# The row turns and queries of tile 1 placed behind the third head's scores, and the first copy of the rows made by ScalarE

## The chip, the cores and the metric

The kernel runs on one core of a Trainium2 chip. The metric is the device time of one launch in microseconds (us), the median of the runs taken; lower is better.

## The reference, cut to what matters

One layer of a decoder for 512 prompt rows and 8 sample rows of width 1024, all in float32: an input projection, a chunked gMLP mixer, a gated linear attention mixer, their merge with a layer norm that gives x1, and then the channel mixer PEER, a second layer norm and a small gated embedding. The part around which the kernel is built is PEER:

```python
q = (xb @ w_q).reshape(blk, PEER_HEADS, 2, half)      # 8 heads of queries, each half normalised
s = jnp.einsum('thpd,hpnd->thpn', q, keys_f)          # scores against 2 x 128 keys per head
s1, i1 = lax.top_k(s[:, :, 0], 16);  s2, i2 = lax.top_k(s[:, :, 1], 16)
sc, ci = lax.top_k(cand, 16)                          # 16 of the 256 sums; idx = expert numbers
h = jax.nn.gelu(jnp.einsum('thkd,td->thk', u_tab[idx], xb))
y = jnp.einsum('thk,thkd->td', softmax(sc) * h, v_tab[idx])
```

Each token takes 16 rows of u_tab and 16 rows of v_tab (4 KB each) for each of 8 heads, so the 512 prompt rows gather 512 x 128 rows from each of two tables of 16384 rows.

## The kernel before, in words

The prompt is four tiles of 128 tokens (0 to 3), the eight sample rows are a fifth (NT = 4). Group 0 is tiles 0 and 1, group 1 is tiles 2, 3 and the samples. The mixers of group 0 run first. Then the PEER stage begins for tile 0, and all that is left of the kernel's dense work (the queries of tile 1, the whole of the mixers of group 1) is dealt out between its steps.

**The plan.** `plan()` writes one list of events, PLAN. TensorE (PE), VectorE (DVE), ScalarE (ACT) and the SyncE queue (SP) each walk this list in order and do their own part of each event; GpSimd (POOL) has a loop of its own that issues the gathers. The PEER stage has one step for each tile and head (`ITERS` = 32 steps), and each step has 16 slots: slot (n, k) of the plan holds `("dots", n + 1, k)`, so a slot (-1, k) is that of dot (0, k). `behind` is the table of the dense work by slot; `spread_over` deals a list of events evenly, by `cost`, over the slots from a first to a last one. `choices_at` gives the slots of the routing of each head: `route` parts 0 and 1 normalise the queries (statistics on DVE, square root and scaling on ACT, lines 868 and 873), `q turn` transposes them on PE (line 1538) and copies them on ACT (line 884), `scores` multiplies by the keys on PE (line 1548) and copies on ACT (line 892), and parts 2 to 6 are top-16, softmax and index arithmetic on DVE.

**A dot.** `dot(n, k)` (line 1280) multiplies 128 gathered rows of u_tab (one per token, 512 KB, one gather of POOL at line 712) by the tile's rows x1 and sums: one DVE instruction. The rows x1 of a tile are first copied into PSUM (`XD`, line 1276, DVE). There are 6 buffers for u rows at first, and two more from dot (1, 3) on; a gather waits (`u_used`) for the dot that last used its buffer. The gathers of v_tab (line 721) have 8 buffers at first; the ninth waits (`v_used`) for the first `sums` event, the PE matmuls (line 1575) that weigh the v rows into Y. That gather stands in POOL's order at (1, 9), ahead of the further u gathers.

**Jobs.** A job is one PE product into one of three PSUM banks `PJ`, with its evacuation by ACT or DVE. Of interest here: `t1` of tile 1 (two jobs of 4 transposes of x1, line 1492, copied by ACT at line 822), `wq` (16 matmuls for one head's queries of a tile, line 1406, copied by ACT at line 805) and the jobs of `mixers(1)` (lines 1514 and 1390 above all). SP loads the weights in a ring of four 1 MB blocks, each load waiting for the last job that uses the block it replaces (line 567); the transposed x of group 1 (line 619) is loaded after job `("job", 0, "wq", 1, 1)`, the second of tile 1's queries.

The part of `plan()` that places the work, up to the change:

```python
close += [e for j in TILES[1] for e in turn(1, "t1", j)]
wq2 = queries(1)
behind = spread_over(wq[3:PH] + turn(0, "t1", 1) + wq[PH:] + mixers(1) + close + wq2[:1], (-1, 0), (13, 6))
```

`wq[3:PH]` are the queries of heads 3 to 7 of tile 0, `turn(0, "t1", 1)` the row turns of tile 1, `wq[PH:]` the eight query jobs of tile 1.

Of the kernel before, what the change touches and what calls it, by code (L numbers as in the profile page):

```python
# [9 lines left out]
ACT = mybir.ActivationFunctionType  # L10
# [10 lines left out]
PH, NK, TOPK = 8, 128, 16  # L21
# [35 lines left out]
def rows(j):  # L57

    return 128 if j < NT else S
# [79 lines left out]
def out_rows(g):  # L139

    return [("job", g, "wo", i, j) for i in range(4) for j in TILES[g]]


def queries(g):

    return [("job", g, "wq", i, j) for i in range(PH) for j in TILES[g]]
# [12 lines left out]
def spread_over(events, first, last):  # L159

    table, total, run = {}, sum(cost(e) for e in events), 0.0
    start = first[0] * TOPK + first[1]
    n = last[0] * TOPK + last[1] - start + 1
    for e in events:
        at = start + min(int(run / total * n), n - 1)
        table.setdefault(divmod(at, TOPK), []).append(e)
        run += cost(e)
    return table


def turn(g, name, j):

    return [("job", g, name, half, j) for half in range(2)]
# [45 lines left out]
def plan():  # L219

    x1 = [[("x1", j, part) for part in range(2)] for j in range(NT + 1)]
    wo = [[("job", 0, "wo", i, j) for i in range(4)] for j in TILES[0]]
    wq = [("job", 0, "wq", i, j) for j in TILES[0] for i in range(PH)]
# [4 lines left out]
    close = out_rows(1) + [e for j in TILES[1] for e in x1[j]]  # L228
    close += [e for j in TILES[1] for e in turn(1, "t1", j)]
    wq2 = queries(1)  # L230
    behind = spread_over(wq[3:PH] + turn(0, "t1", 1) + wq[PH:] + mixers(1) + close + wq2[:1], (-1, 0), (13, 6))
    behind.update(spread_over(wq2[1:], (13, 10), (15, 15)))
    behind.setdefault((END, 10), []).append(("order", NT - 1))
    for k, e in enumerate(spread_norm("norm2")):
# [155 lines left out]
def decoder_step(nc, x_all, x_t, state, p_t, w_blk, w_gkl, w_gk, b_gk, ws_t, ws0, b_s, lnv_g, lnv_b, gn_g,  # L390
                 w_o, ln1_g, ln1_b, w_q, keys_t, u_tab, v_tab, ln2_g, ln2_b, w_pe, w_pg,
                 y_all, st_p, st_s, cv_p, cv_s):
    with ExitStack() as ctx:
        def sem(name):
            return ctx.enter_context(nc.semaphore(name))
# [33 lines left out]
        x1 = at(O_X1, NT + 1, D)  # L429
# [60 lines left out]
        def q_of(j, h):  # L490
# [33 lines left out]
        XD = ctx.enter_context(nc.psum_tensor("XD", [128, 1024], F32))  # L524
# [11 lines left out]
        pj_done, pj_act, pj_dve = sem("pj_done"), sem("pj_act"), sem("pj_dve")  # L536
        soft_part, mid_ok, fac_ok, ent_ok, e_ok, qk_ok = (sem(n) for n in (
            "soft_part", "mid_ok", "fac_ok", "ent_ok", "e_ok", "qk_ok"))
        clear_ok = sem("clear_ok")
        att_ok, s_ok, ms_ok, sdo_ok, on_ok, kpad_ok, qpad_ok, s0_new = (sem(n) for n in (  # L540
            "att_ok", "s_ok", "ms_ok", "sdo_ok", "on_ok", "kpad_ok", "qpad_ok", "s0_new"))
        var_ok, sd_ok, vn_ok, m_ok, x1_ok, x2_ok = (sem(n) for n in ("var_ok", "sd_ok", "vn_ok", "m_ok", "x1_ok", "x2_ok"))
# [214 lines left out]
        def _(act):  # L757
# [164 lines left out]
            for e in PLAN:  # L922
                what, args = e[0], e[1:]
                if what == "job":
                    if e in ACT_DONE:
                        evacuate(e)
                elif what == "soft":
                    soft_logs(*args)
                elif what == "decays":
                    decays(*args)  # L930
                elif what == "rms":
                    j = args[0]
                    p = rows(j)
                    act.wait_ge(ms_ok, j + 1)
                    act.activation(sdO[0:p, :], ss[0:p, j % 2, :], ACT.Sqrt).then_inc(sdo_ok, 1)
                elif what in ("vln", "x1", "x2") and args[1] == 0:
                    p, i = rows(args[0]), int(what == "x2")
                    act.wait_ge(var_ok, LN[what, args[0]] + 1)
                    act.activation(sd[i][0:p, :], mv[i][0:p, 1:2], ACT.Sqrt).then_inc(sd_ok, 1)  # L939
                elif what == "route":  # L940
                    route(*args)
                elif what == "q turn":
                    turned(*args)
                elif what == "scores":
                    take_scores(*args)
                elif what == "gelu":
                    n = args[0]
                    act.wait_ge(h_ok, n + 1)
                    act.activation(hact[:, n % 2, :], hraw[:, n % 2, :], ACT.Gelu_apprx_tanh).then_inc(g_ok, 1)  # L949
                elif what == "spread":  # L950
                    spread(*args)
                elif what == "order":
                    order(*args)
                elif what == "sample dot" and args[0] == S - 1:
                    act.wait_ge(hs_ok, 1)
                    act.activation(aS, hS, ACT.Gelu_apprx_tanh).then_inc(gs_ok, 1)
# [3 lines left out]
        def _(v):  # L960
# [310 lines left out]
            def dot(n, k):  # L1271

                m = u_number(n, k)
                if n % PH == 0 and k == 0:
                    v.wait_ge(x1_ok, n // PH + 1)
                    link(v.tensor_copy(XD[:, :], x1[:, n // PH, :]))
                slot, before, _ = U_PLACE[m]
                v.wait_ge(u_in[slot], 16 * (before + 1))
                t = ubuf[slot]
                v.tensor_tensor_reduce(out=t, in0=t, in1=XD[:, :], scale=1.0, scalar=0.0, op0=ALU.mult,  # L1280
                                       op1=ALU.add, accum_out=hraw[:, n % 2, k:k + 1]).then_inc(u_used, 1)
                if k == TOPK - 1:
                    v.wait_ge(u_used, m + 1)
                    v.sem_inc(h_ok, 1)
# [387 lines left out]
```

## Time and profile before

| what | value |
|---|---|
| time, median of 3 runs | 1904.94 us (1901.7 to 1907.02) |
| the profiled execution's own time | 1903.96 us |
| its span in the profile | 1902.1 us |
| mean granted TensorE clock | 0.833 of full speed |
| busy: PE, DVE, ACT, POOL | 1427.9, 1168.3, 405.6, 995.5 us |
| moved by DMA | 673.22 MB, 545.33 MB of it on the gathers' queue |

The profile cuts the span into 40 slices of 47.6 us each. The dense work of group 0 fills slices 1 to 7, the first gather is issued at 326.26 us, and the last ends shortly after 1864 us. A stretch is best read by its window: busy time of every engine, the granted TensorE clock, the DMA share (mean busy share of the 16 DMA engines) and what they moved per second.

### The profile page before, as it was taken

To read this page: it belongs to the slowest core of one execution; us is meant where nothing else is said; L and a number is where in the kernel's file an instruction comes from. 1 tells how busy PE (TensorE), PEld (TensorE's weight loads), DVE (VectorE), ACT (ScalarE), POOL (GpSimd) and SP (SyncE) were. 2 spreads that over 40 slices of the span, in tenths; PEclk is the share of its full clock that TensorE was granted. 3 is DMA by queue.
4 is the path that set the end of the run, shared out by engine and by line. 5 is a ranking of instruction groups with operands and counts; after the bars stand their busy time and mean duration, and the time that the engine had idled before them with its cause. 6 is when DMAs were issued, how large, how long until landed. Compare 5 with 4: busy or idle time off the path is not lost.

```text
span 1902.1 us, 19841 instructions
## 1 busy us (share of the span) xinstructions
PE 1427.9 (75%) x6728; PEld 890.4 (47%) x6728; DVE 1168.3 (61%) x2989; ACT 405.6 (21%) x829; POOL 995.5 (52%) x1054
## 2 busy tenths in 40 slices
PE   9999998899878798999885895373733445674556
PEld 7888887776654455656552552040400111231113
DVE  1110225878877674766678665878888877766521
ACT  2320201124432121322112121121222111211010
POOL 0000001546655555655575665766667776757761
PEclk9999999999988799989996997575756566586688
DMA  7336551999999999999999999999999999999993
GB/s 289 133 133 224 205 190 53 334 413 403 411 412 410 412 411 405 412 408 393 399 402 394 400 410 412 410 408 397 387 393 409 403 409 373 409 341 409 408 382 149
DMA packets 171889, 673.22 MB, mean 354 GB/s; under 512 B 19423, under 2 KB 22623, under 8 KB 157966
## 3 DMA queue, kind: packets, MB, share of 16 engines
q0 software_dynamic: 149760, 545.33, 72.9%
q1 hardware_dynamic: 22030, 126.63, 17.3%
q8 instruction: 55, 0.90, 0.2%
q14 instruction: 44, 0.36, 0.0%
HBM read 664.48 MB, written 7.41 MB: 353 GB/s over the span
## 4 chain that ended last, share of the span: by engine, by line
PE 38%; DMA 29%; DVE 14%; POOL 11%; issue 6%; ACT 1%; SPq 0%; POOLq 0%; DVEq 0%
DMA at<-in_v_tab,idxV 18%; PE PJ L1514 15%; DMA at<-in_u_tab,idx 10%; PE Y L1575 7%; POOL at L721 6%; DVE at L1280 5%; POOL at L712 5%; PE PJ L1406 5%; PE PJ L1390 3%; PE PJ L1413 3%; DMA at<-in_w_blk 1%; DVE at L1208 1%; PE PJ L1476 1%; PE PJ L1420 0%; PE PJ L1492 0%
## 5 line engine op out<-in xcount | busy, mean ns | idle before, releaser
L712 POOL DMA_INDIRECT at<-in_u_tab,idx x512 | 489.8, 957 | 557.8 <-DVEq L1263 324.0
L1280 DVE CUSTOM_DVE_ANT_0 at<-at,XD 128x1024 f32<-128x1024 f32 x512 | 616.2, 1216 | 219.9 <-DMA at<-in_u_tab,idx 207.4
L1575 PE MATMUL Y<-at,at 128*32 128x512 f32 x2048 | 359.9, 830 | 404.0 <-DMA at<-in_v_tab,idxV 404.0
L721 POOL DMA_INDIRECT at<-in_v_tab,idxV x512 | 487.3, 952 | 306.4 <-PE Y L1575 171.4
L1514 PE MATMUL PJ<-at,at 128*128 128x256 f32 (+1 forms) x1792 | 417.1, 392 | 5.5 <-DVE at L1130 2.3
L1514 PEld LDWEIGHTS PJ<-at,at 128*128 128x128 f32 x1792 | 344.0, 194 | 85.6 <-issue 24.6
L1575 PEld LDWEIGHTS Y<-at,at 128*32 128x32 f32 x2048 | 74.1, 134 | 603.9 <-issue 602.7
L1406 PE MATMUL PJ<-at,at 128*128 128x256 f32 (+2 forms) x960 | 221.5, 390 | 5.8 <-DVE at L1187 4.3
L1406 PEld LDWEIGHTS PJ<-at,at 128*128 128x128 f32 (+2 forms) x960 | 168.4, 178 | 61.7 <-issue 14.4
L1390 PE MATMUL PJ<-at,at 128*128 128x256 f32 (+1 forms) x640 | 142.0, 380 | 0.0
L1390 PEld LDWEIGHTS PJ<-at,at 128*128 128x128 f32 (+1 forms) x640 | 107.6, 170 | 35.9 <-issue 9.1
L1413 PE MATMUL PJ<-at,at 128*128 128x256 f32 (+1 forms) x304 | 72.3, 394 | 7.3 <-issue 6.6
L868 ACT ACTIVATE sdR<-mvR 128x2 f32<-128x2 f32 x34 | 6.9, 203 | 270.4 <-DVE mvR L1224 270.3
L1413 PEld LDWEIGHTS PJ<-at,at 128*128 128x128 f32 (+1 forms) x304 | 53.4, 178 | 23.0 <-issue 7.2
L1183 DVE TENSOR_TENSOR at<-at,PJ 128x256 f32<-128x256 f32 (+1 forms) x16 | 6.8, 425 | 64.0 <-PE PJ L1514 64.0
L1280 DVE DVE_READ_ACCUMULATOR2_ANT hraw<- 128x1 f32 x512 | 42.0, 82 | 0.0
L877 ACT ACT_TABLE_LOAD x32 | 41.1, 1283 | 0.6
L873 ACT ACTIVATE at<-at,mvR,rsR 128x128 f32<-128x128 f32 x68 | 29.7, 484 | 44.7 <-DVE mvR L1229 44.7
L949 ACT ACT_TABLE_LOAD x30 | 38.5, 1283 | 0.5
L939 ACT ACTIVATE sd<-mv 128x1 f32<-128x1 f32 (+1 forms) x15 | 3.0, 203 | 160.6 <-DVE mv L1075 160.6
L892 ACT ACTIVATE at<-R 128x256 f32<-128x256 f32 x34 | 12.9, 380 | 93.8 <-PE R L1548 84.2
L1072 DVE BATCH_NORM_STATS2 bn<-Y 128x6 f32<-128x512 f32 x1 | 0.7, 700 | 52.0 <-PEq L1581 52.0
(213 smaller groups left out, 1316.5 us busy)
## 6 DMA issues: line engine op xcount, KB each, us to landing
at<-in_w_blk SPq DMA_DIRECT2D x72, 1024.0 KB, 7.9
at<-in_w_q SPq DMA_DIRECT2D x16, 1024.0 KB, 8.0
at<-in_w_o SPq DMA_DIRECT2D x8, 1024.0 KB, 8.0
at<-in_u_tab,idx POOLq DMA_INDIRECT x512, 11.5
at<-in_v_tab,idxV POOLq DMA_INDIRECT x512, 11.4
at<-in_state SPq DMA_DIRECT2D x4, 1024.0 KB, 8.4
out_st_s<-at SPq DMA_DIRECT2D x4, 1024.0 KB, 8.5
at<-in_w_pg SPq DMA_DIRECT2D x2, 2048.0 KB, 14.2
```

The lines of the kernel that those rows point to most:

```text
L712: pool.indirect_dma_start(ubuf[slot], None, u_tab, bass.IndirectOffsetOnAxis(rows_of, 0)).then_inc(u_in[slot], 16)
L721: pool.indirect_dma_start(vbuf[slot], None, v_tab, bass.IndirectOffsetOnAxis(rows_of, 0)).then_inc(v_in[slot], 16)
L873: act.activation(half, half, ACT.Identity, scale=rsR[:, i:i + 1], bias=mvR[:, i, 0:1]).then_inc(qn_ok, 1)
L877: act.activation(ex[:, :], top[:, :], ACT.Exp, bias=soft[:, 0:1], accum_out=soft[:, 1:2]).then_inc(exp_ok, 1)
L949: act.activation(hact[:, n % 2, :], hraw[:, n % 2, :], ACT.Gelu_apprx_tanh).then_inc(g_ok, 1)
L1208: link(v.match_replace(src, vals16[:, 0:8], src, NEG))
L1280: v.tensor_tensor_reduce(out=t, in0=t, in1=XD[:, :], scale=1.0, scalar=0.0, op0=ALU.mult, op1=ALU.add, accum_out=hraw[:, n % 2, k:k + 1]). ...
L1390: last = mm(out[0:p, 0:BC], xT[:, k, local(c)], w[:, k, :], start=k == 0, stop=k == KC - 1)
L1406: last = mm(out[0:32 if sample_q else p, 0:256], src[:, k, columns_of], w[:, k % 4, i % 2 * 256:i % 2 * 256 + 256], start=k == 0, stop=k = ...
L1413: last = mm(out[0:p, 0:256], x2T[:, k, 0:p], wpg[i // 2][:, k, i % 2 * 256:i % 2 * 256 + 256], start=k == 0, stop=k == KC - 1)
L1514: last = mm(out[:, 0:ng], w[:, k, 128 * c:128 * c + 128], src[:, k, 0:ng], start=k == 0, stop=k == KC - 1)
L1575: last = mm(Y[32 * c:32 * c + 32, s, :], wpadV[d // PAIR % 2][:, g, :], vbuf[slot][:, 512 * s:512 * s + 512], start=False, stop=final)
```

## The change

Three things change. First, the query jobs of heads 3 to 7 of tile 0 are no longer part of the even spread: they get slots (-1, 0), (-1, 1), (-1, 3), (-1, 5) and (-1, 6), the ones that the spread gave them. Second, the rest of the list (row turns of tile 1, its eight query jobs, `mixers(1)`, `close`, the first query job of group 1) is spread from slot (-1, 13) on, where it went on from slot (-1, 8) before; the last slot (13, 6) stays. `choices_at` puts the third head's (`("route", 0, 2, ...)`) query turn at slot (-1, 11), its scores at (-1, 12) and its first top-16 at (-1, 13), and in one slot the choices stand ahead of `behind`. So the order in PLAN, which was t1 t1, route 0, wq, route 1, q turn, wq, scores, wq, route 2, becomes route 0, route 1, q turn, scores, route 2, t1 t1, wq. Third, the copy of tile 0's rows into `XD` is made by ACT, at the place of event `("route", 0, 1, 2)` in its list (ahead of the query turn of head 1), with a new semaphore `xd_ok` for which dot (0, 0) waits; the copies for tiles 1 to 3 stay on DVE.

```diff
     wq2 = queries(1)
-    behind = spread_over(wq[3:PH] + turn(0, "t1", 1) + wq[PH:] + mixers(1) + close + wq2[:1], (-1, 0), (13, 6))
+    behind = {divmod(m - TOPK, TOPK): [e] for m, e in zip((0, 1, 3, 5, 6), wq[3:PH])}
+    behind.update(spread_over(turn(0, "t1", 1) + wq[PH:] + mixers(1) + close + wq2[:1], (-1, 13), (13, 6)))
     behind.update(spread_over(wq2[1:], (13, 10), (15, 15)))
@@
-        clear_ok = sem("clear_ok")
+        clear_ok, xd_ok = sem("clear_ok"), sem("xd_ok")
@@
                 elif what == "route":
+                    if e == ("route", 0, 1, 2):
+                        act.wait_ge(x1_ok, 1)
+                        act.activation(XD[:, :], x1[:, 0, :], ACT.Copy).then_inc(xd_ok, 1)
                     route(*args)
@@
                 m = u_number(n, k)
-                if n % PH == 0 and k == 0:
+                if (n, k) == (0, 0):
+                    v.wait_ge(xd_ok, 1)
+                elif n % PH == 0 and k == 0:
                     v.wait_ge(x1_ok, n // PH + 1)
                     link(v.tensor_copy(XD[:, :], x1[:, n // PH, :]))
```

## Rows read from the trace of the kernel before

**Rows 1.** The page's 40 slices of 47.6 us: GB/s moved by DMA.
```profile
GB/s 289 133 133 224 205 190 53 334 413 403 411 412 410 412 411 405 412 408 393 399 402 394 400 410 412 410 408 397 387 393 409 403 409 373 409 341 409 408 382 149
```

**Rows 2.** Windows: length, busy PE, PEld, DVE, ACT, POOL, clock, DMA share, GB/s.
```profile
326.00:360.00 34.00, 28.14 (x123) 24.08 (x122) 32.51 (x82) 5.64 (x14) 20.11 (x21) 0.90 0.81 269
...
355.00:360.00 5.00, 4.27 (x13) 3.24 (x12) 4.90 (x14) 1.25 (x3) 3.78 (x5) 0.52 0.96 326
360.00:365.00 5.00, 3.76 (x19) 3.03 (x18) 0.55 (x2) 1.53 (x4) 3.78 (x5) 1.00 1.00 399
...
360.00:480.00 120.00, 117.75 (x581) 85.11 (x583) 91.69 (x248) 39.77 (x90) 69.42 (x73) 1.00 1.02 407
...
850.00:1050.00 200.00, 164.64 (x828) 102.62 (x828) 144.63 (x366) 38.50 (x74) 120.36 (x126) 0.89 1.01 395
1050.00:1870.00 820.00, 466.18 (x2141) 192.68 (x2139) 566.54 (x1465) 149.76 (x299) 565.71 (x598) 0.70 1.01 398
```

**Rows 3.** Waits from 326 to 360 us: GpSimd's u gathers.
```profile
POOL at L712 <- DVE hraw L1280: 9.4, 6, 3.3
```

**Rows 4.** Timeline of VectorE: start, us, instruction, at the first dots.
```profile
330.90 1.33 DVE L1276 COPY XD<-at 128x1024 f32<-128x1024 f32 x1
332.26 1.22 DVE L1280 CUSTOM_DVE_ANT_0 at<-at,XD 128x1024 f32<-128x1024 f32 x1
```

**Rows 5.** Window over the first gathers: GB/s is the last column.
```profile
326.00:331.00 5.00, 5.00 (x25) 4.41 (x24) 4.53 (x21) 0.38 (x1) 3.83 (x4) 1.00 0.52 161
```

**Rows 6.** Timeline of ScalarE where the new copy goes.
```profile
315.81 0.88 ACT L873 ACTIVATE at<-at,mvR,rsR 128x128 f32<-128x128 f32 x2 [0.43 <-DVE mvR L1229]
317.22 0.38 ACT L884 ACTIVATE at<-R 128x256 f32<-128x256 f32 x1 [0.53 <-PE R L1538]
317.62 1.28 ACT L877 ACT_TABLE_LOAD   x1
322.67 0.31 ACT L877 ACTIVATE ex<-top,soft 128x16 f32<-128x16 f32 x1 [3.77 <-DVEq L1243]
```

**Rows 7.** A group of ScalarE by form, whole span: busy us, mean ns.
```profile
L832 ACT ACTIVATE at<-at 128x1024 f32<-128x1024 f32 x1 | 1.1, 1057 | 0.0
```

**Rows 8.** Timeline from 356 to 368 us, TensorE and then VectorE.
```profile
356.52 5.32 PE L1406 MATMUL PJ<-at,at 128*128 128x256 f32 x16 [0.73 <-ACT at L822]
363.07 0.44 PE L1538 MATMUL R<-ident,at 128*128 128x128 f32 x2 [1.24 <-ACT at L873]
363.35 3.62 PE L1406 MATMUL PJ<-at,at 128*128 128x256 f32 x16
366.81 0.61 PE L1548 MATMUL R<-at,at 128*128 128x128 f32 x4
...
356.96 0.16 DVE L1229 SCALAR_TENSOR_TENSOR mvR<-mvR,rsR 128x2 f32<-128x2 f32 x1
...
367.87 0.30 DVE L1206 MAX8 vals<-at 128x8 f32<-128x128 f32 x1 [7.33 <-ACT at L892]
```

**Rows 9.** Waits from 360 to 480 us: who for whom, us in total, times, longest.
```profile
POOL at L712 <- DVE hraw L1280: 27.7, 21, 4.4
...
DVE at L1280 <- DMA at<-in_u_tab,idx: 9.0, 6, 2.3
POOL at L721 <- PE Y L1575: 8.7, 2, 7.5
```

**Rows 10.** Timeline: the loads of SP, and PE's jobs from 388 us on.
```profile
367.00 0.69 SPq L619 DMA_DIRECT2D at<-in_x_t  x1
374.36 14.14 SPq L567 DMA_DIRECT2D at<-in_w_blk  x4
...
388.52 7.36 PE L1514 MATMUL PJ<-at,at 128*128 128x264 f32 x32 [0.17 <-DMA at<-in_w_blk]
...
419.33 1.92 PE L1575 MATMUL Y<-at,at 128*32 128x512 f32 x16
...
421.51 0.94 POOL L721 DMA_INDIRECT at<-in_v_tab,idxV  x1 [7.53 <-PE Y L1575]
```

## The prediction, made before the change was run

> **What bounds the kernel now.** I read the 40 slices of the page first, then windows of the stages they show, then the waits and the timeline where the change acts. In the slices [rows 1] the transfer rate jumps from 53 to 334 GB/s in the eighth slice, where the gathers begin, and from the ninth on stays near 410 until the last: there the kernel is as long as its bytes are many. The windows [rows 2] say it more sharply. From 326 to 360 us the DMA share is 0.81 and the rate 269 GB/s; from 360 to 480 it is 1.02 and 407, from 850 to 1050 1.01 and 395, from 1050 to 1870 1.01 and 398. So the PEER stage has a short mouth of 34 us in which transfers are not the bound, and a body in which they are. 34 x (1 - 269 / 407) = 11.5 us is what the mouth loses against the rate just behind it, the most that any edit there can win. Who holds the transfers back in the mouth is in POOL's waits [rows 3]: 9.4 us in six waits for dots, and VectorE is busy 32.51 of the 34 us [rows 2]. In the mouth VectorE is the bound.
>
> **The first copy of the rows.** VectorE spends 330.90 to 332.26 us on it, 1.33 us of work, and the first dot starts right behind it [rows 4]. With the copy gone the first dot can start at 330.9 if its 128 rows are there. The window from 326 to 331 moved 161 GB/s x 5 us = 0.80 MB [rows 5], more than one gather of 0.52 MB; at the rate of that window's end the second gather is in by about 332, just when dot (0, 1) wants it. So the whole 1.34 us, start to start, comes off VectorE's chain. The lower bound is 0 (a dot that waits for its rows instead), the upper 1.34. I take 1.3. From there on every dot, the layer norm of tile 1 and all gathers that wait for dots come 1.3 us earlier, and the full rate begins 1.3 us earlier: 1.3 us off the end, the transfers behind it being a fixed number of bytes at a fixed rate.
>
> On ScalarE the copy goes between the scaling that ends at 316.69 (315.81 + 0.88) and the turn copy at 317.22 [rows 6]. The nearest row is an ACTIVATE of 128 x 1024, 1057 ns [rows 7], there from SBUF to SBUF. So the copy runs from 316.7 to 317.8 and delays the turn copy, and the table load behind it, by 0.55 us. Who waits for that? The scores of head 1, which on TensorE stand behind a `wo` job of 16 matmuls, 3.6 us like the query job of [rows 8]; and the exponential of head 0, which starts at 322.67 with 3.77 us of idle time before it [rows 6]. 0.55 us fits both; the cost is 0. Were that cover gone it would be 0.55 us.
>
> The Trainium skill (ScalarE: Activation LUTs, Rules for kernel authors) speaks against this edit: simple elementwise work belongs on VectorE, which it calls faster. Its formula for an ACTIVATE with immediate operands (What ACT_TABLE_LOAD costs) gives an estimate of 1.04 us for 1024 columns. By either the rows or the page this copy is no dearer than VectorE's 1.33 us, and the sum is the same, since it lies in ScalarE's idle time.
>
> **The order on TensorE and ScalarE.** Before, tile 1's row turns and its first query job stand ahead of the third head's query turn [rows 8]. TensorE is in that job from 356.52 to 361.84, and ScalarE, whose copy of it (line 805) stands ahead of the scaling, waits although the head's factors were ready at 357.12 (356.96 + 0.16), the turn follows at 363.07, then a second job of 3.62 us stands ahead of the scores at 366.81, and VectorE, which has done dot (0, 13) by 360.54, idles 7.33 us until 367.87. After: factors at 357.12 - 1.3 = 355.8, scaling 0.88, turn 0.44, copy 0.38, scores 0.61, copy 0.38, with some 0.3 us of handing over: 358.8; with TensorE at half clock the turn and scores could cost up to twice that, 359.8. VectorE itself is done with dot (0, 13) at 359.2. So the third head's first MAX8 moves from 367.87 to about 359.5, 8.4 us earlier: 1.3 from the copy, 7.1 from the order.
>
> What of the 7.1 us reaches the end? In the window from 360 to 365, VectorE is busy 0.55 of 5 us, yet POOL is busy 3.78, as in the window before, and the transfers stand at a share of 1.00 and 399 GB/s [rows 2]: the idle stretch costs no bytes while it lasts, because buffers are free and POOL still has gathers to issue. Later POOL waits for dots again, 27.7 us by 480 [rows 9], but with the share at 1.02 over these 120 us the transfers are full all the same, since weights and the x of group 1 fill what gathers leave. A dot that comes earlier only changes whose bytes go first. VectorE waits for u rows 9.0 us in that stretch [rows 9]; that will grow by about what it has gained. So this term is 0, with 7.1 us of gain as its far bound.
>
> **What the order costs.** TensorE's row turns now wait for the scores. Behind them are queued the eight query jobs of tile 1, then all of `mixers(1)`, and on SP the x load, which waits for the second query job, and the weight blocks. Row turns start at about 359, some 5 us later, the first query job at 361.5 instead of 356.52, the second ends at about 369 to 370 instead of 367.0. The first job runs near half clock as it does before (5.32 us against 3.62 for the second [rows 8], granted clock 0.52 from 355 to 360 [rows 2], that is the 1.2 GHz level), TensorE having had nothing to do ahead of it. TensorE is 2 to 3 us behind, the x load goes out at 369.5 instead of 367.00, the first weight block at 377 instead of 374.36 and lands, by the old 14 us [rows 10], at 391; the first job that needs it comes then too. Against that, in the plan every job of group 1 stands 3 to 5 slots later until step 8 and 1 or 2 later until step 13. Six jobs, not eight, of group 1 are ahead of the first `sums`. So that `sums` moves from 419.33 [rows 10] to about 419.3 + 2.7 - 2 x 3.7 = 414.6 (7.36 us for two jobs), and POOL, which stood 7.53 us before the ninth v gather until 421.51, goes on at about 417. It may stand there longer, up to 10 us, since VectorE leads; eight u gathers (4.2 MB) are then in flight, which with a weight block each 7 us last about 16 us, so there is no hole in the transfers. Cost 0 at the start. Then the list's total cost of 519.9 units over 231 slots becomes 500.9 over 218: 2.1% denser. Where transfers set the pace a denser TensorE costs nothing; where TensorE does, it costs 2.1% of the stretch. From 850 to 1050 the rate is 395 and TensorE is busy 164.64 of 200 us at a clock of 0.89 [rows 2]: if a third of that is TensorE's, 1.4 us. Bounds: 0 and 4.2 us. I take 0.3.
>
> The Trainium skill (TensorE: Matmul & The Clock Gate, Why this matters for your kernels) warns against gaps between bursts of matmuls, which put the array back to half clock. By that rule, the trace agrees for the gap before the row turns, and this gap grows with the change. It would make at most two query jobs slow in place of one, 5.32 - 3.62 = 1.7 us more on TensorE alone.
>
> **Sum.** 1903.96 us (span 1902.1 and 1.9 around it) - 1.3 - 0 + 0.3 = 1903.0 for the profiled execution. It is 1.0 below the median of the runs, so 1904.94 - 1.0 = 1903.9; I round to 1903.8. With the far bounds that are all likely inside the case, 1900 to 1907.
>
> **Rivals.**
> - *VectorE's lead reaches the end.* If the body is bound by the chain gather, dot, next gather and only looks full because weights are fetched ahead of need, the 8.4 us stay. For it: POOL's 27.7 us of waits for dots and VectorE as a busy engine at 92 of 120 us [rows 2, 9], and `sums` earlier by 1 to 5 jobs through step 5. Against it: a share of 1.02. Time 1904.94 - 8.4 = 1896.5. Chance 0.17.
> - *TensorE becomes the bound of the mixers.* 2.7 us behind at the start and 2.1% denser over 850 to 1050 is 2.7 + 4.2 - 1.3 = 5.6 slower, 1910.5; over all of 360 to 1050 it is 14.5 + 2.7 - 1.3 = 15.9, 1921. It decides from where the `sums` come so late that POOL's waits for them open holes in the transfers. For it: TensorE 117.75 of 120 us busy from 360 to 480, and waits of POOL for line 1575. Against it: 407 GB/s in that very stretch, and the jobs' later slots. Chance 0.12.
> - *Neither edit does anything.* Dot (0, 0) waits for its rows, the order is hidden: 1904.9. Chance 0.08.
>
> **How the numbers follow.** My forecast, a small gain of about 1 us: 0.63. A change under 0.3%, 5.7 us, is about what a measurement of this kernel can't tell from none; 1899.2 and 1910.7 are these bounds. Below 1899.2 lie the first rival's 0.17 and 0.03 of the forecast, where later dips in the rate shift luckily: faster 0.20. Above 1910.7 lies most of the second rival, slower 0.10. The rest, 0.70, is the same. The range reaches down to the first rival, 1896.5, and up to 1909.
>
> **What would show it.** Right: ACT copy of 128 x 1024 at about 316.7, first dot at 330.9, MAX8 of the third head near 359.5 with no idle time before it, row turns behind the scores, first `sums` near 415, the window from 326 to 360 at about 280 GB/s, from 360 to 480 still 405 to 410, and every later landmark (the first x1 of tile 2, the last gather) some 1 us earlier. Wrong: landmarks at 600 or 1000 us that are 5 us earlier or later, with windows whose rate has changed; a hole in the transfers near 410; a first dot that waits for a gather.

## The result and the profile after

The changed kernel takes 1908.31 us (median of 21 runs, 1902.68 to 1911.99), the kernel before 1902.12 us beside it (21 runs, 1898.76 to 1907.02). The ratio is 1.003 with a 95% interval of 1.0023 to 1.0037: about 6 us slower. I had forecast 1903.8, a gain of 1 us on the 1904.94 us of the first three runs; 21 runs put the kernel before 2.8 us lower. The range I gave, 1896.5 to 1909, holds the time; the direction is wrong. Ratios here are the recorded ones, taken over the fast runs alone (one run each of e10_sums_only and e11_norm was slow, the latter 2664.51 us at a clock of 0.542), so they can differ from the quotient of the two medians.

The profiled execution of after has a span of 1903.2 us and its own time is 1905.15, 3.2 us below the median of its runs, while that of before (1903.96) is 1.8 us above the median of its own. So the two traces are only 1.2 us apart and can't show the whole loss. A second trace of the same kernel (below) has a span of 1911.5.

The early part is what the prediction describes. One thing has to be taken off when the two traces are compared: after's stands 0.9 us earlier before the change acts at all (first gather at 325.35 us, against 326.26). From the timeline of VectorE, at the first dots of after:

```profile
330.04 1.22 DVE L1286 CUSTOM_DVE_ANT_0 at<-at,XD 128x1024 f32<-128x1024 f32 x1
...
332.13 1.22 DVE L1286 CUSTOM_DVE_ANT_0 at<-at,XD 128x1024 f32<-128x1024 f32 x1 [0.87 <-DMA at<-in_u_tab,idx]
```

The copy is gone from VectorE, and the second dot waits 0.87 us for its rows: of the 1.3 us, 0.4 are left (the second dot starts 6.78 us behind the first gather, against 7.15 before). ScalarE's copy, in its own timeline, stands elsewhere than I had put it and than the section on the change says: the event it hangs on, `("route", 0, 1, 2)`, is the first top-16 of head 1, and lies behind the scores of that head, not ahead of its query turn. Nothing waits for it there, and it takes 1.02 us where VectorE took 1.33:

```profile
325.44 1.02 ACT L944 ACTIVATE XD<-at 128x1024 f32<-128x1024 f32 x1
```

The third head's MAX8, the first query jobs of tile 1, the first `sums` and the ninth v gather, each from its engine's timeline, answer to [rows 8, 10]:

```profile
359.65 0.29 DVE L1210 MAX8 vals<-at 128x8 f32<-128x128 f32 x1 [0.38 <-ACT at L893]
...
361.64 17.50 PE L1412 MATMUL PJ<-at,at 128*128 128x256 f32 x80 [0.73 <-ACT at L823]
...
414.38 1.92 PE L1581 MATMUL Y<-at,at 128*32 128x512 f32 x16
...
416.56 0.93 POOL L722 DMA_INDIRECT at<-in_v_tab,idxV  x1 [5.73 <-PE Y L1581]
```

I had said 359.5, 361.5, 415 and 417; with the 0.9 us taken off, the MAX8 comes 7.3 us earlier than before and the `sums` 4.0. One detail differs: I had the first query job near half clock, 5.3 us. It is not: these five jobs take 17.50 us together, 3.5 each. The turn and the scores ahead of them took the half clock (0.69 and 1.22 us against 0.44 and 0.61, granted 0.50 from 355 to 360 us). The windows of after by stage, to set against [rows 2]:

```profile
326.00:360.00 34.00, 24.52 (x113) 21.16 (x112) 31.39 (x82) 6.38 (x16) 20.43 (x22) 0.87 0.84 278
...
360.00:480.00 120.00, 116.16 (x565) 83.10 (x564) 92.61 (x247) 38.13 (x82) 69.71 (x74) 0.98 1.02 410
480.00:850.00 370.00, 321.12 (x1508) 207.02 (x1507) 259.98 (x653) 106.12 (x209) 216.07 (x225) 0.88 1.01 402
850.00:1050.00 200.00, 163.54 (x823) 103.06 (x822) 140.84 (x359) 38.21 (x74) 117.27 (x124) 0.90 1.01 401
1050.00:1870.00 820.00, 460.16 (x2156) 190.63 (x2158) 569.78 (x1471) 150.73 (x302) 569.97 (x601) 0.72 1.01 399
```

The one stage that is worse is 480 to 850 us. For it the kernel before has this row, which the prediction leaves out:

```profile
480.00:850.00 370.00, 315.58 (x1518) 200.25 (x1514) 261.25 (x653) 101.95 (x204) 218.29 (x226) 0.89 1.02 411
```

Nine GB/s less over 370 us is 370 x 9 / 411 = 8.1 us of transfer time. Windows of 10 us tell where. After:

```profile
580.00:590.00 10.00, 10.00 (x48) 5.89 (x47) 9.50 (x24) 0.77 (x2) 6.55 (x7) 0.83 0.93 338
...
660.00:670.00 10.00, 3.80 (x10) 1.22 (x11) 9.16 (x28) 1.70 (x3) 4.70 (x5) 0.50 0.97 367
670.00:680.00 10.00, 10.00 (x49) 6.15 (x48) 2.59 (x5) 7.07 (x13) 0.94 (x1) 0.89 0.79 274
680.00:690.00 10.00, 10.00 (x56) 6.12 (x55) 7.76 (x18) 1.70 (x4) 7.35 (x8) 1.00 0.94 328
```

The same three late windows of the kernel before:

```profile
660.00:670.00 10.00, 10.00 (x53) 6.89 (x52) 9.06 (x27) 7.28 (x13) 5.01 (x6) 1.00 1.02 413
670.00:680.00 10.00, 8.34 (x45) 4.55 (x48) 7.01 (x17) 3.68 (x7) 7.39 (x9) 1.00 1.02 409
680.00:690.00 10.00, 8.88 (x52) 7.17 (x44) 4.27 (x10) 1.15 (x3) 7.26 (x9) 1.00 1.02 413
```

From 660 to 690 us after loses (44 + 137 + 83) / 411 x 10 = 6.4 us against 411 GB/s, at 580 another 1.8. From 850 to 1050 it is after that has the higher rate, 401 against 395 [rows 2], which is 3 us won back. In the worst window VectorE is busy 2.59 of 10 us and POOL issues one gather. What VectorE does there, from its timeline in after:

```profile
665.93 0.17 DVE L1057 COPY qpad<-at 128x8 f32<-128x8 f32 x1
...
670.01 0.16 DVE L1233 SCALAR_TENSOR_TENSOR mvR<-mvR,rsR 128x2 f32<-128x2 f32 x1
673.69 0.16 DVE L1038 TENSOR_SCALAR ss<-ss 8x4 f32<-8x4 f32 x1 [3.52 <-ACT at L862]
677.69 0.17 DVE L1040 RECIPROCAL ss<-sdO 8x4 f32<-8x4 f32 x1 [3.84 <-ACT sdO L936]
677.89 1.21 DVE L1041 TENSOR_TENSOR at<-at,ss 8x1024 f32<-8x1024 f32 x1
679.03 1.20 DVE L1286 CUSTOM_DVE_ANT_0 at<-at,XD 128x1024 f32<-128x1024 f32 x1
```

These are the query, the routing and the norm (event `rms` of tile 4) of the fourth head of the samples' linear attention. TensorE's output job between query and norm, and ScalarE behind it, each from its timeline:

```profile
666.20 6.33 PE L1473 MATMUL PJ<-at,qpad 128*8 128x256 f32 x15 [7.25 <-DVE qpad L1057]
...
672.79 0.37 ACT L859 ACTIVATE at<-PJ 8x256 f32<-8x256 f32 x1 [7.22 <-PE PJ L1473]
...
673.68 1.28 ACT L878 ACT_TABLE_LOAD   x1
...
675.28 0.86 ACT L874 ACTIVATE at<-at,mvR,rsR 128x128 f32<-128x128 f32 x2
676.16 1.28 ACT L936 ACT_TABLE_LOAD   x1
677.45 0.20 ACT L936 ACTIVATE sdO<-ss 8x4 f32<-8x4 f32 x1
```

The chain reads: VectorE copies the query at 665.93; TensorE, 7.25 us idle until then, runs the job at half clock (granted 0.50 in 660 to 670), 6.33 us for 15 of its 16 matmuls; ScalarE takes it at 672.79; VectorE is ready for it at 670.17 and gets it at 673.69. Then VectorE needs a square root, and ScalarE first loads the table of a routing exponential, computes it, scales two factors and loads the table of the root: 3.84 us more. For 7.36 us VectorE does nothing. In the kernel before, the same three places:

```profile
656.63 0.17 DVE L1053 COPY qpad<-at 128x8 f32<-128x8 f32 x1
...
663.49 0.15 DVE L1034 TENSOR_SCALAR ss<-ss 8x4 f32<-8x4 f32 x1
663.94 0.17 DVE L1036 RECIPROCAL ss<-sdO 8x4 f32<-8x4 f32 x1 [0.31 <-ACT sdO L935]
```

There the norm stands 6.9 us behind the query, the job takes 3.61 us (16 matmuls), no other table comes between (ScalarE had just loaded the root's for a routing root), and the wait is 0.31 us. What it does to the gathers stands in POOL's timeline of after:

```profile
668.76 1.11 POOL L713 DMA_INDIRECT at<-in_u_tab,idx  x1 [0.30 <-issue]
674.74 0.94 POOL L722 DMA_INDIRECT at<-in_v_tab,idxV  x1 [4.87 <-PE Y L1581]
680.51 0.94 POOL L713 DMA_INDIRECT at<-in_u_tab,idx  x1 [4.84 <-DVE hraw L1286]
```

From 669.9 us, the end of the first, to 680.5 one gather is issued; the kernel before issues eight in those 10.6 us. POOL is stopped twice, by two engines: first it waits for sums, which stand behind the slow job on TensorE, then for a dot, which stands behind the norm on VectorE.

### The profile page after: what moved, and what is told of

It reads as the page before. It is cut to its first block, busy times and chain, and to the rows that moved or that the text cites. A ratio compares the mean times of both kernels' runs of the same rounds, so it can differ in the third digit from the quotient of the medians.

```text
span 1903.2 us, 19845 instructions
## 1 busy us (share of the span) xinstructions
PE 1423.1 (75%) x6728; PEld 891.0 (47%) x6728; DVE 1167.1 (61%) x2988; ACT 410.2 (22%) x832; POOL 995.7 (52%) x1054
## 4 chain that ended last, share of the span: by engine, by line
PE 40%; DMA 27%; DVE 16%; POOL 10%; issue 7%; ACT 1%; DVEq 0%; POOLq 0%; SPq 0%
DMA at<-in_v_tab,idxV 15%; PE PJ L1520 15%; DMA at<-in_u_tab,idx 11%; PE Y L1581 7%; DVE at L1286 6%; POOL at L722 5%; PE PJ L1396 5%; POOL at L713 5%; PE PJ L1412 4%; PE PJ L1419 3%; DVE at L1212 1%; PE PJ L1467 1%; PE PJ L1473 1%; PE PJ L1482 1%; PE PJ L1489 0%
## 5 line engine op out<-in xcount | busy, mean ns | idle before, releaser
L1581 PE MATMUL Y<-at,at 128*32 128x512 f32 x2048 | 355.6, 821 | 398.6 <-DMA at<-in_v_tab,idxV 398.6
L1544 PE MATMUL R<-ident,at 128*128 128x128 f32 x68 | 16.0, 323 | 26.1 <-ACT at L874 25.3
```

Source lines behind the costliest of these rows:

```text
L1581: last = mm(Y[32 * c:32 * c + 32, s, :], wpadV[d // PAIR % 2][:, g, :], vbuf[slot][:, 512 * s:512 * s + 512], start=False, stop=final)
```

## The experiments

Theories: A, the later and denser slots of `mixers(1)` cost; B, the copy on ScalarE costs; C, the early order costs; D, came with the trace: it is the place of the fourth sample head's block in VectorE's and ScalarE's order; E, the later slots cost in many small places, and the hole at 670 is one execution's accident. The edits are against after and cut to the lines that matter (`...`); where they begin from the plan of before, `behind` is first made by the old call, as in e1_copy, and in e4_late, e6_block, e8_ramp and e11_norm `late` is the table of after.

**e1_copy: the plan of before, ScalarE makes the copy.**

```diff
-    behind = {divmod(m - TOPK, TOPK): [e] for m, e in zip((0, 1, 3, 5, 6), wq[3:PH])}
-    behind.update(spread_over(turn(0, "t1", 1) + wq[PH:] + mixers(1) + close + wq2[:1], (-1, 13), (13, 6)))
+    behind = spread_over(wq[3:PH] + turn(0, "t1", 1) + wq[PH:] + mixers(1) + close + wq2[:1], (-1, 0), (13, 6))
```

> The plan of before with ScalarE's copy of tile 0's rows and nothing else of the change. Theory A (the loss comes from the later and denser slots of the second group's mixers): between 0 and 1.3 us faster than before, 0.4 us by the first gathers of the changed kernel's trace, where dot (0, 1) already waits 0.87 us for its rows. Theory B (the loss is ScalarE's copy, which takes something in the mouth): 6 us slower, like the whole change.

1901.45 against 1901.62 us for the kernel before beside it, ratio 0.9997 (0.9987 to 1.0007). B falls. The copy alone neither costs nor gives anything that can be measured.

**e2_plan: the plan of after, VectorE makes the copy.**

```diff
-                    if e == ("route", 0, 1, 2):
-                        act.wait_ge(x1_ok, 1)
-                        act.activation(XD[:, :], x1[:, 0, :], ACT.Copy).then_inc(xd_ok, 1)
-                if (n, k) == (0, 0):
-                    v.wait_ge(xd_ok, 1)
-                elif n % PH == 0 and k == 0:
+                if n % PH == 0 and k == 0:
```

> The change of the plan alone, VectorE makes all four copies. Theory A: 6 us slower than before, as much as the whole change. Theory B: no slower than before.

1908.37 against 1901.62, ratio 1.0043 (1.0028 to 1.0058), with the waits of 3.8 and 3.3 us at the norm and 358, 295, 317 GB/s in the three windows from 660. The whole loss is the plan's.

**e3_order: the early order of after, the mixers in the slots of before.**

```diff
+    for at in [at for at, events in behind.items() if any(e in wq[PH:] or e in turn(0, "t1", 1) for e in events)]:
+        behind[at] = [e for e in behind[at] if e not in wq[PH:] and e not in turn(0, "t1", 1)]
+    for k, e in zip((13, 13, 13, 14, 14, 15, 16, 17, 19, 21), turn(0, "t1", 1) + wq[PH:]):
+        behind.setdefault(divmod(k - TOPK, TOPK), []).append(e)
```

> The changed kernel, but every job of mixers(1) and behind it keeps the slot that it has before the change; only the row turns and the eight queries of tile 1 move behind the third head's scores, crowded into slots (-1, 13) to (0, 5). Theory A (later slots): same as before or up to 2 us faster, no hole in the transfers at 670 us. Theory C (the order on TensorE and ScalarE itself costs, since TensorE is 3 us late into a stretch in which it has no idle time): 4 to 7 us slower.

1903.98 against 1901.62, ratio 1.0009 (0.9997 to 1.002). No hole from 660 to 690, but one at 420. As many jobs stand ahead of the first `sums` as before (eight of group 1, where after has six), but TensorE begins tile 1's queries at 361.43 us in place of 356.52, so the `sums` are late, while POOL arrives early because VectorE leads. A window of it, and POOL's timeline:

```profile
420.00:430.00 10.00, 10.00 (x50) 5.01 (x50) 8.07 (x29) 2.26 (x4) 4.68 (x5) 1.00 0.81 282
```

```profile
424.04 0.94 POOL L725 DMA_INDIRECT at<-in_v_tab,idxV  x1 [13.33 <-PE Y L1584]
```

A wait of 13.3 us for sums opens a hole (282 GB/s) where one of 7.5 [rows 10] or 5.7 did not (411 and 410 in the same window).

**e4_late: the early order of before, the mixers in the slots of after.**

```diff
+    late = spread_over(turn(0, "t1", 1) + wq[PH:] + mixers(1) + close + wq2[:1], (-1, 13), (13, 6))
+    early = wq[3:] + turn(0, "t1", 1)
+    behind = {at: [e for e in events if e in early] for at, events in behind.items()}
+    for at, events in late.items():
+        behind[at] = behind.get(at, []) + [e for e in events if e not in early]
```

> The changed kernel, but the row turns and queries of tile 1 keep the slots and the order that they have before the change; mixers(1) and all behind it have the changed kernel's slots, 4 later at first. Theory A: 5 to 7 us slower, with windows at 570 to 590 and 660 to 690 us that fall to 270 to 370 GB/s. Theory C: same as before within 1 us.

1911.81 against 1901.62, ratio 1.0059 (1.0044 to 1.0073). It is as slow as after or slower, so the early order is not needed for the loss, and A holds: the slots are what costs. C falls as the cause of the 6 us; that the early order costs one or two us by itself is not excluded (e3_order). The norm waits 2.1 and 3.8 us here, and there are windows of 290 GB/s at 470, 358 at 580, 346 at 680 and 355 at 790. The trace is of the fastest of the six runs, 1906.64 us, and can't account for the other half of the 10 us.

**e5_rms: after, with the sample norm alone moved back behind dot (7, 7).**

```diff
+    behind = {at: [e for e in events if e != ("rms", NT)] for at, events in behind.items()}
+    behind.setdefault((6, 7), []).insert(0, ("rms", NT))
```

> The changed kernel with one event moved: the samples' output norm (rms of tile 4) goes from behind dot (7, 2) to behind dot (7, 7). Theory D (most of the loss is VectorE standing at that norm, with no dots and so no gathers, for the fourth sample head's output and two table loads of ScalarE): the windows from 660 to 690 us go back to 400 GB/s and more, and the time falls by 4 to 6 us, to within 2 us of before. Theory E (the later slots cost in many small places and that hole is one execution's accident): at most 2 us faster than the changed kernel.

1905.68 against 1902.71, ratio 1.0022 (1.0011 to 1.0032). The wait did not go, it moved along, because ScalarE's root stands in order behind copies of later jobs. From the timelines of VectorE, TensorE and POOL:

```profile
686.18 0.17 DVE L1042 RECIPROCAL ss<-sdO 8x4 f32<-8x4 f32 x1 [7.64 <-ACT sdO L938]
...
665.18 6.21 PE L1475 MATMUL PJ<-at,qpad 128*8 128x256 f32 x15 [8.31 <-DVE qpad L1059]
...
673.60 0.94 POOL L724 DMA_INDIRECT at<-in_v_tab,idxV  x1 [4.75 <-PE Y L1583]
...
686.32 0.93 POOL L724 DMA_INDIRECT at<-in_v_tab,idxV  x1 [3.10 <-PE Y L1583]
```

and the windows that hold the two:

```profile
670.00:680.00 10.00, 10.00 (x53) 6.80 (x51) 5.67 (x15) 6.25 (x11) 4.87 (x6) 0.95 0.87 318
680.00:690.00 10.00, 10.00 (x59) 5.75 (x58) 3.78 (x7) 4.18 (x7) 5.42 (x6) 1.00 1.01 402
```

402, 318 and 402 GB/s in the windows from 660 lose 2.7 us in place of 6.4. This parts the two stops of POOL. The hole that is left, at 670, lies ahead of VectorE's wait (678.5 to 686.2): it comes with POOL's 4.75 us of waiting for the sums behind the half-clock job. VectorE's 7.64 us, as long as both waits in after, fall in a window of 402 GB/s, 0.2 us lost; POOL had issued eight gathers in a row from 673.60 on. So here a late norm cost little with many gathers in flight, and in after much, with POOL just stopped by something else. What is left of the ratio has further holes beside it, 356 GB/s at 580 and 352 at 790, and the trace is of the fastest of the nine runs.

**e6_block: the order of before and the copy, with the fourth sample head, its outer products, output job and norm, and the two jobs that follow, in the slots of after.**

```diff
+    block = [("head", 3)] + [("job", 1, "outer", 3, c) for c in range(4)] + [("query", 3), ("job", 1, "os", 3, NT), ("rms", NT),
+                                                                               ("job", 1, "gb", 1, 1), ("job", 1, "va", 0, 2)]
+    behind = {at: [e for e in events if e not in block] for at, events in behind.items()}
+    for at, events in late.items():
+        behind[at] = [e for e in events if e in block] + behind.get(at, [])
```

> The plan of before with ScalarE's first copy, and only the fourth sample head (its outer products, query, output and the norm behind it, with two jobs that must stay in order) in the changed kernel's slots. Theory D: the hole at 660 to 690 us is there (270 to 360 GB/s in three windows), 4 to 6 us slower than before. Theory E: no slower than 1 us.

1907.54 against 1902.71, ratio 1.0029 (1.0014 to 1.0044). Moving these few events two or three slots, and nothing else beside the copy (e1_copy: no effect), gives the loss of the whole change. VectorE's waits from 560 to 700 us:

```profile
DVE ss L1045 <- ACT sdO L941: 3.8, 1, 3.8
DVE ss L1043 <- ACT at L867: 3.4, 1, 3.4
```

and the windows of the hole:

```profile
650.00:660.00 10.00, 8.20 (x32) 3.89 (x32) 5.13 (x10) 0.00 (x0) 4.67 (x4) 0.67 0.96 371
660.00:670.00 10.00, 2.06 (x5) 0.66 (x6) 9.15 (x28) 1.70 (x3) 4.47 (x5) 0.50 0.77 264
670.00:680.00 10.00, 10.00 (x46) 5.35 (x45) 2.63 (x8) 5.52 (x11) 2.24 (x3) 0.82 0.85 298
680.00:690.00 10.00, 10.00 (x48) 6.92 (x46) 7.06 (x15) 2.98 (x5) 6.08 (x7) 1.00 0.89 286
```

The hole is deeper than after's, 9.4 us from 660 to 690 against 6.4; its time is the same within the intervals.

**after_again: the changed kernel, one more trace.**

> The changed kernel once more, for its trace. Theory D: the hole between 660 and 690 us is there again. Theory E: holes of the same size stand elsewhere.

One run, 1913.44 us, with 388, 306 and 293 GB/s from 660 and waits of 3.4 and 3.8 us. Place and size repeat.

**e7_head3: after, with the fourth head put back against the dots and the routing.**

```diff
+    outer = [("job", 1, "outer", 3, c) for c in range(4)]
+    block = [("head", 3)] + outer + [("query", 3), ("job", 1, "os", 3, NT), ("rms", NT)]
...
+    for at, events in (((5, 12), block[:2]), ((5, 13), block[2:4]), ((5, 14), block[4:6]), ((5, 15), block[6:7]), ((6, 0), block[7:])):
+        behind[at] = behind.get(at, []) + events
```

> The changed kernel, with the fourth sample head (outer products, query, output) and the norm behind it put back where they stand before the change against dots and routing: query behind dot (6, 14), output behind (6, 15), norm behind (7, 0) and ahead of the activation of step 6. All other events of the mixers keep the changed kernel's slots. Theory D: VectorE's two waits at the norm, 7.3 us, shrink under 2 us, the windows from 660 to 690 us are at 400 GB/s, and the kernel is 4 to 6 us faster than the changed one, 0 to 2 us slower than before. Theory E: no more than 2 us of the 6 come back.

1903.99 against 1900.85, ratio 1.0013 (1.0004 to 1.0022). The root's wait is down to 1.5 us, but the outer products, back in their own slots while the jobs ahead of them are still two or three slots late, now hold VectorE (waits from 560 to 700 us), and there is a hole of 277 GB/s at 660:

```profile
DVE at L1150 <- PE PJ L1472: 20.3, 5, 10.0
```

About half of the loss is gone, and the hole that is left has another wait beside it: the norm is one instance of a kind, not the only possible one.

**e8_ramp: every event 0 to 4 slots later, the delay of after at step 1 shrinking to none by step 4.**

```diff
+    was, then = ({e: TOPK * n + k for (n, k), events in t.items() for e in events} for t in (behind, late))
+    behind = {}
+    for e, at in was.items():
+        weight = min(max((72 - then.get(e, at)) / 56, 0), 1)
+        at = at + int(weight * (then.get(e, at) - at) + 0.5)
+        behind.setdefault(divmod(at, TOPK), []).append(e)
```

(`was` and `then` are the slots of before and of after.)

> The changed kernel, but the delay of the mixers' slots shrinks from 4 slots at step 1 to none at step 4, so that from there on the plan is that of before. The first sums have six jobs ahead of them as in the changed kernel, the sample heads stand as before. If both holes found so far (at 670 us from the sample norm, at 425 us where POOL stands before the ninth v gather because eight jobs are ahead of the first sums) are the whole cost, this is as fast as before or up to 2 us faster. If being later and denser costs by itself, it is 2 us or more slower than before, with new holes between 430 and 550 us.

1907.11 against 1900.85, ratio 1.003 (1.0018 to 1.0042). The fourth head is back in its slot and its wait gone. Denser steps 1 to 4 made a new one there, a third place, with 258 and 321 GB/s in the windows from 520 and 530. VectorE's waits from 500 to 550 us:

```profile
DVE at L1121 <- PE PJ L1458: 9.4, 1, 9.4
```

**e9_sums and e9_sums_again: e3_order with the last two k jobs moved behind the first `sums`; e10_sums_only: the same two jobs moved in e1_copy.**

```diff
+    for e, k in ((("job", 1, "k", 1, 0), 3), (("job", 1, "k", 1, 1), 4)):
+        behind = {at: [x for x in events if x != e] for at, events in behind.items()}
+        behind[1, k] = [x for x in behind.get((1, k), []) if x[:3] == ("job", 1, "k")] + [e] + [
+            x for x in behind.get((1, k), []) if x[:3] != ("job", 1, "k")]
+    behind[1, 4].insert(1, ("job", 1, "low", 0))
+    behind[1, 3].remove(("job", 1, "low", 0))
```

> The kernel in which only the order changed and the mixers kept their slots, with two jobs (the last two of k) moved one to three slots later, behind the first sums, so that six jobs are ahead of them and not eight. The hole at 420 to 430 us should be gone. If VectorE's lead of 7 us from the new order is worth anything once no hole eats it: 2 to 7 us faster than before. If the body is bound by its bytes: within 1.5 us of before.

> ScalarE's first copy and the plan of before with the same two jobs behind the first sums; the row turns and queries of tile 1 stay where they are before. Control for the run beside it: within 1.5 us of before by both theories, since the wait of POOL before the ninth v gather there opened no hole in the transfers.

> The same kernel as the one with the early order of after, the mixers in the slots of before and the last two k jobs behind the first sums, timed once more. If lost transfer time is all that counts, it is like the kernel before, 0.999 to 1.000, with no hole at 420 to 430 and none at 660 to 690. If the early order has a price of its own that the hole at 420 to 430 did not explain, 1.001 or more.

These runs, and the two below, fell in conditions in which the kernel before takes 2005 to 2011 us (their traces have 356 to 367 GB/s from 1050 to 1870 us, against 398 [rows 2]), and a third of a per cent is hard to see. e9_sums: 2011.47 against 2005.03, ratio 1.0031 (1.0 to 1.0062); again 2008.98 against 2005.13, 1.0019 (1.0 to 1.0037). e10_sums_only: 2000.6 against 2005.03, 0.9986 (0.9953 to 1.0019). POOL's wait for the first sums is still 12.7 us in e9, against 8.0 in e10, so the edit did not do what it was for. The hole at 420 to 450 is still there in e9 (317, 347, 228 GB/s), but e10, without the early order, has one too (369, 389, 199), so under these conditions it tells nothing. From 640 to 690 e9 is full, 410 to 417 GB/s. Nothing here speaks for the early order being a gain.

**e11_norm and e11_norm_again: e6_block without the head and its outer products, so that only query, output job and norm (and the two jobs) are late.**

```diff
-    block = [("head", 3)] + [("job", 1, "outer", 3, c) for c in range(4)] + [("query", 3), ("job", 1, "os", 3, NT), ("rms", NT),
+    block = [("query", 3), ("job", 1, "os", 3, NT), ("rms", NT),
```

> The order of before and ScalarE's first copy; of the fourth sample head only its query, its output sums and the norm (with the two jobs behind it) stand in the slots of after, three slots later, right behind one another across a routing exponential. The head itself and its four outer products stay where they were before. If the wait at the norm alone makes the loss (theory D), VectorE waits some 3.5 + 3.8 us at the norm, as in after, the transfers have a hole near 670 of some 5 us, and the ratio is 1.003. If the loss is the outer products' waits and the norm together, the norm's waits are there, but gathers have been issued farther ahead, the hole is 2 to 3 us, and the ratio is 1.001 to 1.002. If the norm's wait is harmless by itself, the ratio is that of the copy alone, 1.000, and the head and outer products in after's slots are what costs.

> The same kernel as the one with the query, output sums and norm of the fourth sample head alone in the slots of after, timed once more. In its first trace VectorE waited 2.6 + 3.8 us at the norm, but the transfers lost only some 2.7 us, at 690 to 710 us. If the norm's wait alone is the loss (theory D), the ratio is 1.003; if it is the outer products' waits and the norm together, 1.001 to 1.002; if the norm alone is harmless, 1.000.

2020.52 against 2011.28, ratio 1.0016 (0.9987 to 1.0045; the medians alone would give 1.0046), and 2009.01 against 2005.13, 1.0016 (0.9997 to 1.0035). By time neither run tells 1.000 from 1.003. The second trace does tell something. VectorE waits 3.1 and 3.8 us at the norm, and the windows are

```profile
680.00:690.00 10.00, 7.08 (x31) 2.47 (x32) 6.38 (x21) 2.56 (x7) 4.27 (x5) 0.60 1.03 409
690.00:700.00 10.00, 10.00 (x48) 8.11 (x44) 5.87 (x14) 7.25 (x11) 3.51 (x4) 1.00 0.93 344
700.00:710.00 10.00, 10.00 (x60) 5.49 (x59) 4.45 (x11) 1.14 (x3) 5.90 (x8) 1.00 0.97 355
```

a hole of (67 + 56) / 411 x 10 = 3.0 us, where e9 under the same conditions has none. In the first trace it is 2.7 us. So the late query, output job and norm by themselves go with about half of the 6.4 us. That the outer products' waits ahead of them, which leave fewer gathers in flight, are the other half is not shown: it is an inference from e6_block less e11_norm, taken under different conditions, and the second trace of e11_norm also has a hole of 246 GB/s at 760 that after's first trace has not.

**One sum over all traces.** For each profiled execution I added up (411 - rate) / 411 over the 10 us windows from 360 to 1870 us:

| kernel | lost, 360 to 850 | 850 to 1050 | whole, 360 to 1870 | that execution's own time, us |
|---|---|---|---|---|
| before | 1.5 | 8.0 | 34.8 | 1903.96 |
| e1_copy | 0.8 | 10.4 | 35.3 | 1901.78 |
| e5_rms | 5.5 | 5.8 | 35.8 | 1903.78 |
| e3_order | 5.8 | 4.9 | 37.6 | 1907.18 |
| e4_late | 7.6 | 5.5 | 37.6 | 1906.64 |
| after | 8.3 | 4.8 | 37.7 | 1905.15 |
| e2_plan | 9.2 | 4.4 | 38.2 | 1907.60 |
| e7_head3 | 7.9 | 5.6 | 38.9 | 1906.31 |
| e8_ramp | 5.9 | 8.5 | 39.5 | 1907.11 |
| e6_block | 11.0 | 3.9 | 40.4 | 1908.46 |
| after_again | 11.8 | 4.5 | 42.7 | 1913.44 |

Over 8 us of lost transfer time the own time rises by some 10, with a scatter of about 2 us. The columns also show that part of a hole is filled again. Before and e1_copy have dips of their own between 850 and 1050 us, 8.0 and 10.4 us, and every kernel with holes ahead of 850 has shallower ones there, by 2 to 4 us, except e8_ramp. So after is 6.8 us behind before by 850 and 2.9 by 1870. Why the dips shrink no run shows.

## Why the prediction was wrong, by its own steps

**What bounds the kernel.** Right in the main, and it is also what made the loss: from 360 us on the time is bytes over rate, so a hole in the transfers is time. But "near 410 until the last" read too much into the slices [rows 1], which have 373 and 341 among them. The body of before loses 8 us between 850 and 1050 and 25 behind, and that slack takes up part of a new hole.

**The copy, 1.3 us.** Right in mechanism, mis-sized. 0.4 us are left after the second dot's wait, and e1_copy measures 0.2 us with an interval of about 2 us to either side. I had weighed bytes moved by 331 us; the row to weigh was when the second gather lands. That ScalarE's copy costs nothing was right, but not for the reason given: it does not run at 316.7 us, with 0.55 us of delay behind it, but at 325.44, in an idle stretch of 4 us.

**The early order, 0.** Right as to the gain. MAX8 at 359.65, first `sums` at 414.4, and 410 GB/s from 360 to 480: VectorE's lead is spent waiting, and the first rival (the lead reaches the end, 0.17) is refuted. e4_late, which lacks the early order and has the late slots, is no faster than after.

**What the order costs, 0.3 us. This step failed.** I wrote that "where transfers set the pace a denser TensorE costs nothing", and priced the later slots by their density, 2.1%, in the one stage where I thought TensorE might be the bound. From 850 to 1050 nothing was lost (4.8 us of transfer time against 8.0 before). The cost arose from 480 to 850, a stage in which the kernel before has 411 GB/s and for which my sum has no term, and not through TensorE's load but through order. VectorE takes some results of the mixers in line with its dots, and TensorE has the sums in line behind the mixers' jobs. A query copied late by VectorE left TensorE idle, the job behind it ran at half clock, the sums behind that job stopped POOL, and the norm, 7 us late, stopped the dots and POOL again. The measured size is about 6 us (ratios 1.003 for after, 1.0043, 1.0059 and 1.0029 for the three kernels with the late block). The first trace has 6.4 us in the hole from 660 to 690 and 1.8 at 580 (there VectorE waits 3.3 us, until 576.36, for a state load that is also later, and POOL for a dot until 580.00), of which 3 are won back by 1050. The shift was not a rigid one either: I had written 3 to 5 slots until step 8, but by the plans it is 4 at first, and at the block, in steps 5 and 6, three for the query and two for the output job and the norm, so neighbours in the list moved against the dots and the routing by different amounts.

**The slower rival.** Its criterion was half right (it decides where POOL's waits for sums open holes; that was one of the two stops) and its place and mechanism were wrong: it had TensorE's throughput as a bound. Its mild form gave 5.6 us more than before, close to the 6.2 measured, by another cause. That is luck.

**The clock.** That TensorE falls behind by a gap showed twice. At 356.82 it had been idle 9.01 us and took 0.69 us for a turn of 0.44, but no query job was slow, where I had allowed for one or two. At 666.20 it had been idle 7.25 us and took 6.33 us for 15 matmuls where before took 3.61 for 16. The Trainium skill (TensorE: Matmul & The Clock Gate, Why this matters for your kernels) warns of such gaps, and the trace agrees; I had applied it only to the gap that I could see in the diff's neighbourhood.

**Small slips.** The rows give 1.36 us from the copy's start to the first dot's, not 1.34, and the sum ends at 1903.9, not 1903.8; neither matters.

**What stays open.** How the loss divides between outer products, slow job and norm was seen only in single traces, e5_rms's and, under other conditions, e11_norm's. Nor was it settled what the early order with untouched late slots would be worth if no `sums` were delayed: e3_order and the two runs of e9_sums lie at 1.0009, 1.0031 and 1.0019, with intervals that reach down to 1.000. No version that beats the kernel before was found.

## What to carry to other kernels

When a list of events is re-dealt, density is the wrong thing to compare: for each result that the pacing engine (here VectorE, whose dots free the gather buffers) takes in order, compare the distance in time between the instruction that starts it and the one that takes it, before and after, with every hand-over, table load and half-clock job between. A shift of two or three slots far from the edit turned a wait of 0.3 us into 7.4 here. Where transfers are the bound, look at short windows for holes, and at each for which wait of the issuer opened it: here there were two, and moving the later one (e5_rms) left the earlier.

## What the runs showed that I had not expected

How far the transfers carry the kernel over a stop of their issuer depends on what is in flight: 5.7 us of POOL's waiting for sums at 415 us cost nothing and 7.5 at most 0.9 us (387 and 398 GB/s from 430 on), in both cases after u gathers that had waited for a free buffer, so with all of these in use; 13.3 us opened a hole in which (129 + 32 + 39) / 411 x 10 = 4.9 us were lost by 450 us (282, 379 and 372 GB/s in e3_order), and two waits of 4.9 and 4.8 us with one gather between them lost 6.4 us.

A change of ScalarE's table costs the load alone here: the load starts at 673.68 and the exponential at 674.97, 1.29 us later, the copy ahead of the load having ended at 673.66. The Trainium skill (ScalarE: Activation LUTs, What ACT_TABLE_LOAD costs) adds a drain of about 1.38 us to a load of 1.28; this trace agrees on the load and shows no drain.
